# A fused two-block network on one core: the recurrence and gate columns of the second mixing stage transposed by DMA in 16-bit planes

## The chip, the cores and the metric

The program runs on one core of one Trainium2 chip. The engines in play are TensorE (matrix products and transposes), ScalarE, VectorE, GpSimd, the sync engine SP, which issues nearly all DMAs, and the 16 DMA engines of the core. The metric is the device time of one execution in microseconds (us), lower is better.

## The reference

Two transformer-like blocks run one after the other on an activation of 256 tokens by 1024 columns, all in float32. The second block is the one that matters here:

```python
h = rmsnorm_2(x, norm_mix_g)
proj = h @ w_in                                     # 1024 -> 7168 columns
q, k, v, xr, gr, g_attn, g_rnn = split(proj)        # 1024 columns each
attn_out = diff_attention(q, k, v, ...)             # 8 heads, then a norm by head
xc = conv_b + sum(xpad[:, tap:tap + S] * conv_w[tap] for tap in range(4))
r = sigmoid(blockdiag(xc, w_a) + b_a); i = sigmoid(blockdiag(xc, w_x) + b_x)
a = exp(-8 * r * softplus(-lru_lambda))
hs = scan(h_t = a_t * h_(t-1) + sqrt(1 - a_t^2) * i_t * xc_t)
rnn_out = hs * gelu(gr)
merged = sigmoid(g_attn) * (attn_out @ w_proj_attn) + sigmoid(g_rnn) * (rnn_out @ w_proj_rnn)
x = x + merged @ w_out
x = x + relu(rmsnorm_2(x) @ w_up)^2 @ w_down
```

The convolution and the scan run along the tokens. They are computed with the columns on the 128 partitions and the tokens along the free side, so `xr` and `gr`, which the projection leaves with tokens on the partitions, have to be transposed: 1024 columns each, in 128x128 blocks of 32-bit numbers.

## The kernel before

**Weights.** All weights stream through three slots, `raw[0..2]`, of 1 MB each; a slot's content is a unit, n. A float32 product is made of three reduced-precision products: ScalarE rounds `raw` to `hi`, VectorE writes `lo = raw - hi`, and TensorE adds up `xh*hi + xh*lo + xl*hi`. SP issues the load of unit n when `lo_done` shows that unit n - 3 has been split.

**The second mixing stage** is a loop over steps p = 0 to 55, written out once for each engine. Every chunk c of 512 projected columns has four steps, p = 4c to 4c + 3: two halves u of the contraction by two tiles t of 128 tokens. In each step TensorE does one `portion`, 12 matmuls of 512 columns. In the last two steps of a chunk (u = 1) ScalarE evicts the result bank `G[t]`. Chunks 0 and 3 are q, 1 and 4 are k, 2 and 5 are v, 6 and 7 the recurrence input, 8 and 9 its gate, 10 to 13 the output gates. Other work is attached to fixed steps by tables (`M2_T`, `M2_STEP`, `M2_RI`, `M2_SUB`, `M2_OUT_T`): each engine works through its own list in the order of p, and semaphores hold it where it depends on another.

**The transposes.** `M2_T` gives key (c, t) the step 4(c + 1) + 1 + t, so chunk 6 is transposed at steps 29 and 30, chunk 9 at 41 and 42. ScalarE first evicts chunk c into `hid[:, t]` (line 1105). At the step of the key, TensorE turns four 128x128 blocks of `hid` against an identity into bank `X[0]` (line 2120, a group of four), and ScalarE evicts that bank to `xrt` (lines 1066 to 1068, chunks 6 and 7) or `grt` (1070, chunks 8 and 9), counting `k_trev`.

**What hangs on them.** GpSimd computes the convolution, block b of 128 columns after block (lines 705 to 720): one scaling with bias (711), then three times a scaling into `rg` and an addition into `xc` (715, 716). It starts at `k_trev` 10, that is when both tiles of chunk 6 are in `xrt`, and needs `k_trev` 12 for blocks 4 to 7. After each block it counts `k_xc`. TensorE multiplies block b with `wax` at step 37 + b (lines 2167, 2168), so the eighth at step 44, and ScalarE makes the two sigmoids and a tanh out of it. GpSimd then computes `ig * xc` for five blocks (724), the powers that make the reciprocal roots of the attention output norm (728), and the last three products. VectorE scales `xn`, the attention output, with these (line 1679, two halves; `k_on`), TensorE transposes it from step 47 on (2177), and ScalarE and VectorE split it to `oth` and `otl`.

**Attention** runs beside this up to step 38: TensorE's scores (1930 to 1934), VectorE's bias, maximum and, two steps later, normalisation (`logits`, 1364 to 1368; 1643 to 1652), ScalarE's exponentials (1114).

**The feed-forward stages** already turn their hidden tiles by DMA: VectorE writes the high and the low 16 bits of `hid` as two planes (line 1257), SP issues a transposing DMA for each token tile (line 490), and VectorE merges the planes into 32-bit numbers (line 1265).

## Time and profile before

| | |
|---|---|
| median of 3 runs | 1007.38 us (1006.54 to 1007.86) |
| the profiled execution | 1006.67 us, span 1004.9 us |
| TensorE busy | 996.3 us (99%) |
| VectorE busy | 680.4 us (68%) |
| ScalarE busy | 545.8 us (54%) |
| GpSimd busy | 114.7 us (11%) |
| HBM read | 182.45 MB, 187 GB/s over the span with what is written |

All times in the profile count from the start of the span. In a timeline row the first number is the start, the second the duration; matmuls are pipelined, so each lasts longer than the distance to the start of the next, and distances between starts tell what a piece of TensorE's list costs. In brackets stands how long the engine had been idle and who released it. SPq rows are DMA issues. The second mixing stage lies between about 575 and 763 us, its steps 26 to 47 between 658 and 734.

### The profile page before, as it was taken

What the parts mean: (1) busy time and instruction counts of PE and PEld (TensorE: products, weight loads), DVE (VectorE), ACT (ScalarE), POOL (GpSimd) and SP (SyncE); (2) the same over time, 40 slices, a digit from 0 to 9 for tenths busy, and PEclk for the clock granted to TensorE, in tenths of its full rate; (3) what the DMA queues carried; (4) which work ended last, traced back from release to release, by engine and by line L of the source; (5) the groups of instructions that cost most, each with busy time, mean ns of one, the idle gap of its engine ahead of it and who ended that gap; (6) DMA issues with size and microseconds to landing.
All of it is one profiled execution on the core that took longest, in us unless ns stands there. A gap on an engine that the chain in (4) does not pass through costs nothing.

```text
span 1004.9 us, 12613 instructions
## 1 busy us (share of the span) xinstructions
PE 996.3 (99%) x4658; PEld 817.6 (81%) x4658; DVE 680.4 (68%) x1000; ACT 545.8 (54%) x749; POOL 114.7 (11%) x109
## 2 busy tenths in 40 slices
PE   8999999999999999999999999999999999999998
PEld 7788888888777888888888877888888888888887
DVE  6656666668977667656666668766589767656663
ACT  7444344566765546444343576766875545444441
POOL 0000000022200000000000041219923000000000
PEclk9999999999999999999999999999999999999999
DMA  8977776585434536666756376535346546787761
GB/s 266 297 241 253 238 243 213 188 302 178 129 128 138 194 127 213 225 204 207 222 187 227 123 257 210 161 133 168 126 168 209 183 156 216 231 222 228 223 196 42
DMA packets 150505, 197.77 MB, mean 197 GB/s; under 512 B 41137, under 2 KB 96570, under 8 KB 150330
## 3 DMA queue, kind: packets, MB, share of 16 engines
q1 hardware_dynamic: 150442, 197.15, 60.7%
q8 instruction: 29, 0.48, 0.2%
q14 instruction: 18, 0.15, 0.0%
q10 hardware_dynamic: 16, 0.00, 0.0%
HBM read 182.45 MB, written 5.77 MB: 187 GB/s over the span
## 4 chain that ended last, share of the span: by engine, by line
PE 93%; DVE 3%; DMA 1%; ACT 1%; POOL 1%; issue 0%; SPq 0%; ACTq 0%
PE bank L1775 22%; PE bank L1777 22%; PE bank L1776 22%; PE bank L1880 7%; PE bank L1878 7%; PE bank L1879 7%; PE bank L1788 1%; DMA raw<-in_w_in 1%; PE bank L1930 1%; PE bank L2032 1%; DVE lo L1214 1%; PE bank L2120 1%; POOL rstd_q L682 1%; PE bank L1945 0%; DMA resid<-in_x 0%; DVE ss_q L1478 0%
## 5 line engine op out<-in xcount | busy, mean ns | idle before, releaser
L1775 PE MATMUL bank<-hi,xh 128*128 128x512 f32 (+1 forms) x944 | 375.4, 398 | 1.4 <-DVE xl L1236 0.8
L1777 PE MATMUL bank<-hi,xl 128*128 128x512 f32 (+1 forms) x944 | 367.2, 389 | 0.0
L1776 PE MATMUL bank<-lo,xh 128*128 128x512 f32 (+1 forms) x944 | 366.7, 388 | 0.0
L1197 DVE TENSOR_TENSOR lo<-raw,hi 128x2048 fp32r<-128x2048 f32 x112 | 256.2, 2289 | 147.8 <-ACT hi L756 147.8
L756 ACT ACTIVATE hi<-raw 128x2048 fp32r<-128x2048 f32 (+1 forms) x116 | 220.5, 1902 | 132.9 <-PE bank L1880 96.9
L1775 PEld LDWEIGHTS bank<-hi,xh 128*128 128x128 f32 x944 | 177.5, 188 | 40.4 <-issue 2.3
L1777 PEld LDWEIGHTS bank<-hi,xl 128*128 128x128 f32 x944 | 177.3, 188 | 37.4
L1776 PEld LDWEIGHTS bank<-lo,xh 128*128 128x128 f32 x944 | 177.6, 188 | 34.4
L1214 DVE TENSOR_TENSOR lo<-raw,hi 128x1024 fp32r<-128x1024 f32 (+1 forms) x108 | 133.3, 1241 | 42.4 <-ACT hi L765 41.9
L1878 PE MATMUL bank<-hi,hh 128*128 128x512 f32 x304 | 118.9, 391 | 0.0
L1880 PE MATMUL bank<-hi,hl 128*128 128x512 f32 x304 | 118.4, 389 | 0.0
L1879 PE MATMUL bank<-lo,hh 128*128 128x512 f32 x304 | 118.3, 389 | 0.0
L765 ACT ACTIVATE hi<-raw 128x1024 fp32r<-128x1024 f32 x100 | 103.9, 1050 | 15.5 <-PE bank L1777 11.2
L830 ACT ACTIVATE hh<-hid_t 128x512 fp32r<-128x512 f32 x34 | 20.7, 629 | 92.5 <-DVE hid_t L1265 89.4
L1880 PEld LDWEIGHTS bank<-hi,hl 128*128 128x128 f32 x304 | 57.1, 188 | 11.9
L1879 PEld LDWEIGHTS bank<-lo,hh 128*128 128x128 f32 x304 | 57.1, 188 | 11.7
L1878 PEld LDWEIGHTS bank<-hi,hh 128*128 128x128 f32 x304 | 57.1, 188 | 11.5
L818 ACT ACTIVATE act_out<-bank,small 128x256 f32<-128x256 f32 x44 | 20.9, 476 | 56.4 <-PE bank L1777 53.5
L675 POOL TENSOR_TENSOR small<-small 128x1 f32<-128x1 f32 x10 | 8.5, 848 | 371.6 <-DVE small L1221 353.4
L682 POOL TENSOR_TENSOR rstd_q<-ss_q,small 128x8 f32<-128x8 f32 x16 | 37.4, 2336 | 90.7 <-DVE ss_q L1480 90.7
L1273 DVE TENSOR_TENSOR hl<-hid_t,hh 128x512 fp32r<-128x512 f32 x34 | 22.9, 691 | 20.8 <-ACT hh L830 20.8
L1248 DVE SCALAR_TENSOR_TENSOR hid<-bank,small,act_out 128x256 f32<-128x256 f32 x44 | 21.1, 481 | 15.3 <-ACT act_out L818 15.3
(257 smaller groups left out, 948.5 us busy)
## 6 DMA issues: line engine op xcount, KB each, us to landing
raw<-in_w_in SPq DMA_DIRECT2D x48, 1024.0 KB
raw<-in_ffn_w_gu SPq DMA_DIRECT2D x84, 512.0 KB
raw<-in_ffn_w_down SPq DMA_DIRECT2D x22, 1024.0 KB
raw<-in_w_up SPq DMA_DIRECT2D x16, 1024.0 KB
raw<-in_w_down SPq DMA_DIRECT2D x16, 1024.0 KB
raw<-in_w_out SPq DMA_DIRECT2D x8, 1024.0 KB
distance_table<-ftab SPq DMA_DIRECT2D x8, 576.0 KB
raw<-in_w_proj_attn SPq DMA_DIRECT2D x4, 1024.0 KB
```

The source lines that it names most:

```text
L682: nc.gpsimd.tensor_tensor(rstd_q[:, s], ss_q[:, s], minus_half[:, 0:8], ALU.pow).then_inc(rstd_sem, 1)
L756: nc.scalar.activation(hi[s][:, :, 0:width], raw[s][:, :, 0:width], ACT.Copy).then_inc(hi_done, 1)
L765: ins = nc.scalar.activation(hi[s][:, cut, :], raw[s][:, cut, :], ACT.Copy)
L1197: nc.vector.tensor_tensor(lo[s][:, :, 0:width], raw[s][:, :, 0:width], hi[s][:, :, 0:width].bitcast(F32), ALU.subtract).then_inc(lo_done, 1)
L1214: ins = nc.vector.tensor_tensor(lo[s][:, cut, 0:width], raw[s][:, cut, 0:width], hi[s][:, cut, 0:width].bitcast(F32), ALU.subtract)
L1273: nc.vector.tensor_tensor(hl[:, kt, :], hid_t[:, kt, :], hh[:, kt, :].bitcast(F32), ALU.subtract).then_inc(f.hl, 1)
L1775: nc.tensor.matmul(o, sh, wh, start=first and j == 0, stop=False)
L1776: nc.tensor.matmul(o, sh, wl, start=False, stop=False)
L1777: ins = nc.tensor.matmul(o, sl, wh, start=False, stop=last and j == 3)
L1878: nc.tensor.matmul(DB[t][h][:, :], sh, wh, start=begin, stop=False)
L1879: nc.tensor.matmul(DB[t][h][:, :], sh, wl, start=False, stop=False)
L1880: ins = nc.tensor.matmul(DB[t][h][:, :], sl, wh, start=False, stop=end)
```

## The change

For chunks 6 to 9 the transposes no longer go through TensorE. ScalarE, after evicting `hid[:, t]` and after the step's weight split, copies it once more as 16-bit elements, the low halves into one plane and the high halves into the other (`planes_of`: blocks 4 to 7 of `ig`, which are not in use yet, and `v2` for chunk 9). SP issues one transposing DMA for each tile, before the second weight load of chunk c + 3. At the step where TensorE had its group, VectorE merges the two transposed planes into `xrt` or `grt`, and counts `k_trev`. Where buffers are used again new waits order it: SP waits for the merge of the chunk before, ScalarE for it before it writes the planes of chunks 7 and 8, and before it overwrites `sq` at step 39. Three semaphores go; two were never waited for, and the wait of VectorE on itself that used the third now uses VectorE's general step counter. Left out of the diff below are their declarations.

```diff
+def by_dma(c):
+    return 6 <= c < 10
+def merged_before(c, t):
+    return 8 + 2 * (c - 7) + t + 1
+        def planes_of(c, t):
+            words = v2[:, t, 0:W] if c == 9 else ig[:, 4 + 2 * t:6 + 2 * t, :].rearrange("p b c -> p (b c)")
+            return words.bitcast(U16)
+        def turned_planes_of(c, t):
+            words = (k_2[:, 2 * t:2 * t + 2, :].rearrange("p b c -> p (b c)") if c == 9
+                     else sq if t == 0 else late_t[:, :])
+            return words.bitcast(U16).rearrange("p (k c) -> p k c", c=P)
...
 # SP
+            def flip_mixed(c):
+                for t in range(NT):
+                    sp_eng.wait_ge(k_planes, 2 * (c - 6) + t + 1)
+                    if c > 6:
+                        sp_eng.wait_ge(k_trev, merged_before(c, t))
+                    sp_eng.dma_start_transpose(turned_planes_of(c, t), planes_of(c, t)).then_inc(k_flip[t], 16)
+
             for c, (first, _) in enumerate(IN2):
                 for half in range(2):
+                    if half == 1 and by_dma(c - 3):
+                        flip_mixed(c - 3)
                     columns(a["w_in_2"], U_M2 + 2 * c + half, first, half)
...
 # ScalarE
-                if key is not None:
+                if key is not None and not by_dma(key[0]):
...
-                    elif cc < 8:
-                        nc.scalar.activation(xrt[:, 4 * (cc - 6):4 * (cc - 6) + 4,
-                                                 TAPS - 1 + tt * P:TAPS - 1 + (tt + 1) * P],
-                                             view, ACT.Copy).then_inc(k_trev, 1)
-                    else:
-                        nc.scalar.activation(grt[:, 4 * (cc - 8):4 * (cc - 8) + 4, rows], view,
-                                             ACT.Copy).then_inc(k_trev, 1)
...
                     elif kind in "xr":
-
-                        act.wait_ge(k_tr, 8 + 2 * (c - 6) + t - 1)
+                        if c == 6:
+                            act.wait_ge(k_tr, 7 + t)
                         nc.scalar.activation(hid[:, t, :], G[t][:, :], ACT.Copy, scale=rstd).then_inc(k_ev, 1)
...
                     act.wait_ge(k_oev, NH)
+                    if m == 0:
+                        act.wait_ge(k_trev, 14)
...
                 mixing_split(split_hi_part, U_M2, p)
+                if u == 1 and by_dma(c):
+                    act.wait_ge(k_ev, 2 * c + t + 1)
+                    if c in (7, 8):
+                        act.wait_ge(k_trev, merged_before(c, t))
+                    nc.scalar.activation(planes_of(c, t).rearrange("p (s c) -> p s c", s=2),
+                                         hid[:, t, :].bitcast(U16).rearrange("p (c s) -> p s c", s=2),
+                                         ACT.Copy).then_inc(k_planes, 1)
...
 # VectorE
+                key = key_at(M2_T, p)
+                if key is not None and by_dma(key[0]):
+                    cc, tt = key
+                    dve.wait_ge(k_flip[tt], 16 * (cc - 6) + 16)
+                    dst = (xrt[:, 4 * (cc - 6):4 * (cc - 6) + 4, TAPS - 1 + tt * P:TAPS - 1 + (tt + 1) * P] if cc < 8
+                           else grt[:, 4 * (cc - 8):4 * (cc - 8) + 4, tt * P:(tt + 1) * P])
+                    nc.vector.tensor_copy(dst.bitcast(U16).rearrange("p k (c s) -> p s k c", s=2),
+                                          turned_planes_of(cc, tt).rearrange("p (s k) c -> p s k c", s=2)
+                                          ).then_inc(k_trev, 1)
                 mixing_split(split_lo_half, U_M2, p)
...
 # TensorE
-                if key is not None:
+                if key is not None and not by_dma(key[0]):
...
-                    if cc < 6:
-                        pe.wait_ge(k_qn, 2 * (0, 1, 3, 4).index(cc) + tt + 1)
-                    else:
-                        pe.wait_ge(k_ev, 2 * cc + tt + 1)
+                    pe.wait_ge(k_qn, 2 * (0, 1, 3, 4).index(cc) + tt + 1)
```

VectorE's list at steps 29 and 30, in the old program. The first two rows are the end of step 29's combining; `lo<-raw,hi` are half splits of a weight unit, ISA the logits' custom operation and its read of the maximum.

```order
L1652 SCALAR_TENSOR_TENSOR l<-l,small 128x256 [waits dve_step]
L1652 SCALAR_TENSOR_TENSOR l<-l,small 128x128
L1214 TENSOR_TENSOR lo<-raw,hi 128x1024 [waits hi_half]
L1364 ISA l,small<-bank,bias 128x256 [waits k_pt,k_s]
L1364 ISA small 128x1
L1364 ISA l,small<-bank,bias 128x128
L1364 ISA small 128x1
L1368 TENSOR_SCALAR small<-small 128x2 [waits dve_step]
L1214 TENSOR_TENSOR lo<-raw,hi 128x1024 [waits hi_done]
```

The same place in the new program (its line numbers are 33 or 34 higher):

```order
L1685 SCALAR_TENSOR_TENSOR l<-l,small 128x256 [waits dve_step]
L1685 SCALAR_TENSOR_TENSOR l<-l,small 128x128
L1727 COPY xrt<-act_out 128x2x4x128 [waits k_flip0]
L1248 TENSOR_TENSOR lo<-raw,hi 128x1024 [waits hi_half]
L1398 ISA l,small<-bank,bias 128x256 [waits k_pt,k_s]
L1398 ISA small 128x1
L1398 ISA l,small<-bank,bias 128x128
L1398 ISA small 128x1
L1402 TENSOR_SCALAR small<-small 128x2 [waits dve_step]
L1727 COPY xrt<-late_t 128x2x4x128 [waits k_flip1]
L1248 TENSOR_TENSOR lo<-raw,hi 128x1024 [waits hi_done]
```

Each of the two steps has a merge into `xrt` in front of its half split. The second has the logits of step 30 in front of it.

ScalarE's list from step 26's second exponential to step 28's split, in the old program (`pt`, `xn`: evictions of attention tiles; `hid`: the eviction of chunk 6; `hi`: half splits):

```order
L1114 ACTIVATE l,small<-l,small 128x128
L765 ACTIVATE hi<-raw 128x1024
L1080 ACTIVATE xn<-bank 128x2x128 [waits k_pv]
L1105 ACTIVATE hid<-bank,small 128x512 [waits k_tr,used]
L1114 ACTIVATE l,small<-l,small 128x256 [waits k_l]
L1114 ACTIVATE l,small<-l,small 128x128
L765 ACTIVATE hi<-raw 128x1024 [waits used,raw_in1]
L1114 ACTIVATE l,small<-l,small 128x256 [waits k_l]
L1114 ACTIVATE l,small<-l,small 128x128
L765 ACTIVATE hi<-raw 128x1024
```

And in the new one:

```order
L1137 ACTIVATE l,small<-l,small 128x128
L796 ACTIVATE hi<-raw 128x1024
L1173 ACTIVATE ig<-hid 128x1024 [waits k_ev]
L1103 ACTIVATE xn<-bank 128x2x128 [waits k_pv]
L1128 ACTIVATE hid<-bank,small 128x512 [waits k_tr,used]
L1137 ACTIVATE l,small<-l,small 128x256 [waits k_l]
L1137 ACTIVATE l,small<-l,small 128x128
L796 ACTIVATE hi<-raw 128x1024 [waits used,raw_in1]
L1173 ACTIVATE ig<-hid 128x1024 [waits k_ev]
L1137 ACTIVATE l,small<-l,small 128x256 [waits k_l]
L1137 ACTIVATE l,small<-l,small 128x128
L796 ACTIVATE hi<-raw 128x1024
```

Two rows `ig<-hid` are new, each behind a half split, and all later rows move back by one and by two.

On SP four pairs of transposing DMAs now stand in the stream of loads, each pair between two loads: the first pair between those of units 18 and 19 of the stage, the next after every second load. On GpSimd nothing is moved.

## Rows read from the trace of the kernel before

**Rows 1.** The page, parts 1 and 2: engines; clock in 40 slices.

```profile
PE 996.3 (99%) x4658; PEld 817.6 (81%) x4658; DVE 680.4 (68%) x1000; ACT 545.8 (54%) x749; POOL 114.7 (11%) x109
PEclk9999999999999999999999999999999999999999
```

**Rows 2.** TensorE in order of time: start us, us, engine, line, tiles; [idle before].

```profile
580.39 0.39 PE L1775 MATMUL bank<-hi,xh 128*128 128x512 f32 x1
...
583.11 0.39 PE L1775 MATMUL bank<-hi,xh 128*128 128x512 f32 x1
...
683.76 0.60 PE L2120 MATMUL bank<-ident,hid 128*128 128x128 f32 x4
...
686.96 0.60 PE L2120 MATMUL bank<-ident,hid 128*128 128x128 f32 x4
```

**Rows 3.** GpSimd in order of time, steps 30 to 47.

```profile
673.72 0.55 POOL L711 TENSOR_SCALAR xc<-xrt,cols 128x256 f32<-128x256 f32 x1 [33.37 <-ACT xrt L1066]
...
722.26 5.53 POOL L724 TENSOR_TENSOR ig<-ig,xc 128x256 f32<-128x256 f32 x5
727.75 2.91 POOL L728 TENSOR_TENSOR rstd_q<-ss_q,small 128x16 f32<-128x16 f32 x1
```

**Rows 4.** VectorE in order of time, the scaling of `xn`.

```profile
730.69 3.44 DVE L1679 TENSOR_TENSOR xn<-xn,rstd_q 128x1024 f32<-128x1024 f32 x2 [1.26 <-POOL rstd_q L728]
```

**Rows 5.** TensorE in order of time, steps 44 and 47.

```profile
724.78 0.59 PE L2167 MATMUL bank<-xc,wax 128*128 128x256 f32 x2
...
733.85 0.60 PE L2177 MATMUL bank<-ident,xn 128*128 128x128 f32 x4
```

**Rows 6.** ScalarE in order of time, steps 27 and 28.

```profile
662.56 0.39 ACT L1080 ACTIVATE xn<-bank 128x256 f32<-128x256 f32 x1 [0.54 <-PE bank L2155]
...
666.12 1.05 ACT L765 ACTIVATE hi<-raw 128x1024 fp32r<-128x1024 f32 x1
```

**Rows 7.** VectorE in order of time, steps 28 to 30.

```profile
667.20 1.23 DVE L1214 TENSOR_TENSOR lo<-raw,hi 128x1024 fp32r<-128x1024 f32 x1 [0.31 <-ACT hi L765]
...
669.35 0.42 DVE L1364 CUSTOM_DVE_ANT_0 l<-bank,bias 128x256 f32<-128x256 f32 x1 [0.92 <-PE bank L1934]
...
672.96 0.42 DVE L1364 CUSTOM_DVE_ANT_0 l<-bank,bias 128x256 f32<-128x256 f32 x1
...
673.63 0.17 DVE L1368 TENSOR_SCALAR small<-small 128x2 f32<-128x2 f32 x1
```

**Rows 8.** Line 1265, the feed-forward stages' merge: ns min/median/max.

```profile
L1265 DVE COPY hid_t<-halves_t x27: 744/748/1345, 29.5 to 972.4; 128x1024 uint16<-128x1024 uint16 x20, 128x2048 uint16<-128x2048 uint16 x7
```

**Rows 9.** SP's queue: one load; line 490, the feed-forward transposing DMAs.

```profile
663.31 0.39 SPq L462 DMA_DIRECT2D raw<-in_w_in  x1
...
L490 SPq DMA_TRANSPOSE halves_t<-halves x54: 1188/1201/4111, 23.8 to 964.0; - x54
...
DMA to landing us min/median/max: 2.3/2.3/6.6
```

**Rows 10.** Two conv lines, then groups by line, 673 to 723 us: busy, mean.

```profile
L715 POOL TENSOR_SCALAR rg<-xrt,cols x24: 476/480/1532, 674.2 to 721.0; 128x256 f32<-128x256 f32 x24
...
L716 POOL TENSOR_TENSOR xc<-xc,rg x24: 725/739/1781, 674.8 to 721.6; 128x256 f32<-128x256 f32 x24
...
L716 POOL TENSOR_TENSOR xc<-xc,rg 128x256 f32<-128x256 f32 x24 | 21.5, 898 | 2.0
L715 POOL TENSOR_SCALAR rg<-xrt,cols 128x256 f32<-128x256 f32 x24 | 17.3, 719 | 1.6
L711 POOL TENSOR_SCALAR xc<-xrt,cols 128x256 f32<-128x256 f32 x8 | 6.5, 810 | 33.4 <-ACT xrt L1066 33.4
...
L1214 DVE TENSOR_TENSOR lo<-raw,hi 128x1024 fp32r<-128x1024 f32 x14 | 19.4, 1395 | 17.4 <-ACT hi L765 17.4
...
L1648 DVE TENSOR_SCALAR l<-l,small 128x256 f32<-128x256 f32 (+1 forms) x4 | 2.4, 646 | 0.1
L1652 DVE SCALAR_TENSOR_TENSOR l<-l,small 128x256 f32<-128x256 f32 (+1 forms) x4 | 2.1, 573 | 0.1
```

More of the change, by code:

```diff
@@ L287, in program @@
                 pt2 = sb("pt2", [P, 2, SPAN], F32, s2)
+                late_t = sb("late_t", [P, W], F32, s2)
             with scope() as s2:
@@ L366, in program @@
         m_causal = sem("m_causal")
-        m_sel = sem("m_sel")
         m_masked = sem("m_masked")
@@ L391, in program @@
         k_trev = sem("k_trev")
+        k_planes = sem("k_planes")
+        k_flip = [sem(f"k_flip{t}") for t in range(NT)]
         k_s = sem("k_s")
@@ L410, in program @@
         k_spexp = sem("k_spexp")
-        k_sp = sem("k_sp")
-        k_pad = sem("k_pad")
         k_xc = sem("k_xc")
@@ L699, in _ @@
             pool.wait_ge(n_var, 8)
-            nc.gpsimd.memset(xrt[:, :, 0:TAPS - 1], 0.0).then_inc(k_pad, 1)
+            nc.gpsimd.memset(xrt[:, :, 0:TAPS - 1], 0.0)
             norm_rstd(3)
@@ L1059, in _ @@
                     rows = slice(tt * P, (tt + 1) * P)
-                    if cc < 6:
-                        dst = q_2 if cc in (0, 3) else k_2
-                        g = C_GAIN + (4 if cc in (0, 3) else 5)
-                        nc.scalar.activation(dst[:, 4 * (cc // 3):4 * (cc // 3) + 4, rows], view, ACT.Copy,
-                                             scale=cols[:, g:g + 1]).then_inc(k_trev, 1)
-                    elif cc < 8:
-                        nc.scalar.activation(xrt[:, 4 * (cc - 6):4 * (cc - 6) + 4,
-                                                 TAPS - 1 + tt * P:TAPS - 1 + (tt + 1) * P],
-                                             view, ACT.Copy).then_inc(k_trev, 1)
-                    else:
-                        nc.scalar.activation(grt[:, 4 * (cc - 8):4 * (cc - 8) + 4, rows], view,
-                                             ACT.Copy).then_inc(k_trev, 1)
+                    dst = q_2 if cc in (0, 3) else k_2
+                    g = C_GAIN + (4 if cc in (0, 3) else 5)
+                    nc.scalar.activation(dst[:, 4 * (cc // 3):4 * (cc // 3) + 4, rows], view, ACT.Copy,
+                                         scale=cols[:, g:g + 1]).then_inc(k_trev, 1)
                 for h in range(NH):
@@ L1544, in _ @@
                 if p == M1_TOPK + TOPK // 8:
-                    nc.vector.tensor_scalar(score[:, :], score[:, :], (FILL + TAKEN) / 2, NEG,
-                                            ALU.is_gt, ALU.mult).then_inc(m_sel, 1)
+                    step(nc.vector.tensor_scalar(score[:, :], score[:, :], (FILL + TAKEN) / 2, NEG,
+                                                 ALU.is_gt, ALU.mult))
                 h = at(M1_MASK, p)
@@ L1551, in _ @@
                     if h == 0:
-                        dve.wait_ge(m_sel, 1)
                         dve.wait_ge(bias_a_in, 32)
@@ L1627, in _ @@
                     nc.vector.tensor_scalar(sp[:, 2, :], y, -LRU_C, None, ALU.mult)
-                    nc.vector.tensor_scalar(sp[:, 3, :], y, LRU_C, None, ALU.mult).then_inc(k_sp, 1)
+                    nc.vector.tensor_scalar(sp[:, 3, :], y, LRU_C, None, ALU.mult)
                 k = at(M2_STEP, p)
@@ L2114, in _ @@
                         pe.wait_ge(k_trev, order)
-                    if cc < 6:
-                        pe.wait_ge(k_qn, 2 * (0, 1, 3, 4).index(cc) + tt + 1)
-                    else:
-                        pe.wait_ge(k_ev, 2 * cc + tt + 1)
+                    pe.wait_ge(k_qn, 2 * (0, 1, 3, 4).index(cc) + tt + 1)
                     for j in range(4):
```

## The prediction, made before the result was known

> **What bounds the kernel now.** I read the page first: TensorE is busy for 99% of the span at a granted clock of 1.00 throughout [rows 1], so any instruction taken off it is worth its issue time as long as nothing else ends later. Then TensorE's own order of time, for the price of a group of four transposes: between the starts of two groups with twelve matmuls between them lie 686.96 - 683.76 = 3.20 us, and twelve matmuls without a group take 583.11 - 580.39 = 2.72 us [rows 2]. A group costs 0.48 us. Next I looked for chains that run beside TensorE and are close behind it. One stands out: GpSimd's convolution of the recurrence columns. It begins when the last `xrt` tile of column chunk 6 is there (673.72), runs eight blocks back to back until 722.26, goes on with five products, takes the powers for the output norm (727.75 to 730.66) [rows 3], and VectorE scales `xn` with them at once (730.69, two halves in 3.44 us, so the first is done at about 732.4) [rows 4]. TensorE reads the last conv block at 724.78 and the first half of `xn` at 733.85, both without a wait [rows 5]. So the chain from the eighth block to `xn` has 2.5 us of slack at step 44 and only 733.85 - 732.4 = 1.4 us at step 47. GpSimd has no free time in between: nothing of TensorE's gain can pass it unless GpSimd starts or runs earlier too.
>
> **The change part by part.**
>
> *TensorE.* Eight groups (chunks 6 to 9, two token tiles) go, at steps 29 to 42: 8 x 0.48 = 3.8 us less in its queue before step 44. This is all that the edit can give, 1006.67 - 3.8 = 1002.9 us for the profiled execution.
>
> *ScalarE.* Eight evictions of X[0] go and eight copies of 128x1024 16-bit elements come. No row shows such a copy on ScalarE; I take 1.05 us, the time of a split of 128x1024 in 32 bits [rows 6], with 0.5 us (half, were it to go by bytes) and 2.1 us (double) as ends. I let the next instruction follow 0.95 us after such a copy's start (an estimate, a little under its length). In steps 26 and 27 they come before anything is taken away: the only free time there is the 0.54 us before 662.56 [rows 6], so the first copy pushes by 0.4, the second by its 0.95, and the split of step 28 moves from 666.12 to about 667.45, ending at 668.5. VectorE's second half of that split (667.20 before, 1.23 long [rows 7]) then ends near 669.7, and the logits queued behind it start there and not at 669.35: +0.35 us. TensorE's scores for them are half a microsecond earlier and don't matter.
>
> *VectorE.* Eight merging copies come. The same copy in the feed-forward stages, 128x1024 in 16 bits, takes 0.75 us [rows 8]. The copy for (6, 0) stands before the first split of step 29, that for (6, 1) behind the logits of step 30, which began with the row at 672.96 and ended at 673.80 [rows 7]. Both lie in front of GpSimd's start, and this was the point where the old path had the TensorE group and a ScalarE eviction, started in parallel with those logits. New start: 673.80 + 0.35 + 2 x 0.75 + 0.05 for the signal = 675.7, against 673.72: **+2.0 us**. The ends are +1.2 (ScalarE's copies hidden) and +3.2 (copies of double length on ScalarE).
>
> *SP and the DMA engines.* The two transposing DMAs of a chunk stand before the second weight load of chunk c + 3. For chunk 6 the load before them is issued at 663.31 [rows 9], the first one right behind it at 663.7; the second when its planes are there, about 666.7. In the feed-forward stages an issue takes 1.2 to 4.1 us and the landing comes 2.3 to 6.6 us after it [rows 9]. With the worst of these the tiles are there at 670.3 and 673.3, before their merges at 672.3 and 674.9. The load behind them waits for the split of step 28 anyway (end 669.7) and is used five steps later. I cost the DMAs at nothing; the cover is 1.6 to 2.0 us, and each microsecond beyond it goes straight into GpSimd's start, because the split and the logits queue behind the waiting merge.
>
> *GpSimd beside VectorE.* Its 56 conv instructions would take 24 x 0.48 + 24 x 0.74 + 8 x 0.55 = 33.7 us at their undisturbed lengths; they took 17.3 + 21.5 + 6.5 = 45.3, so 11.6 us were lost. In the same stretch VectorE's splits, and its scaling and combining of `l`, all on SBUF, took 19.4 + 2.4 + 2.1 = 23.9 us [rows 10]: GpSimd lost 0.49 us for each. Six merges fall in that stretch (chunks 7 to 9), 6 x 0.75 = 4.5 us, which at 0.49 is **+2.2 us**. The ends are 0 (a one-input copy disturbs nothing) and +4.5 (each stops GpSimd for its whole length). The Trainium skill, SBUF — State Buffer, "Who interferes with whom", speaks against the change here: a VectorE copy in a two-port mode takes the port pair that GpSimd uses, for the whole instruction, and the other side stands still. The trace agrees in kind: GpSimd instructions of 0.48 us at the least last up to 1.53 [rows 10]. By the letter of that rule the term would be up to 4.5 and the time up to 1012.5 us.
>
> *The sum.* The first half of `xn` is ready at 732.4 + 2.0 + 2.2 = 736.6 and not at 732.4; TensorE wanted it at 733.85 before and would want it at 730.1 now. It starts step 47's transposes at 736.6, 2.8 us later than before, after about 6.6 us of waiting, spread over the reads of conv blocks 5, 6 and 7 (steps 42 to 44) and step 47. From there on everything keeps its distance to TensorE: VectorE's splits of steps 45 and 46 come right behind the scaling, and TensorE needs them three steps on, at least 3 x 2.72 = 8.2 us later. So 1006.67 + 2.8 = 1009.5 for an execution like the profiled one (its span of 1004.9 and 1.8 around it). The median of the three shown is 0.7 above that one, so I forecast 1007.38 + 2.8 = **1010.2 us**. The dropped semaphores and the ScalarE wait of step 39 for chunk 8's merges (queued at step 38 on VectorE, which was idle before its split) cost nothing that I can find.
>
> **Rivals.**
>
> *A. The full gain reaches the end*: 1007.4 - 3.8 = 1003.6, faster. It needs GpSimd's chain to be earlier by 3.8 - 1.4 = 2.4 us where I have it later by 4.2. For it speaks only that TensorE is the bound by every total; against it, that the chain starts behind a merge which stands behind logits, and that VectorE has no slot to make up time. It decides if the merge of (6, 1) is done before 671.3, before those logits.
>
> *B. GpSimd is late by little, and its slack covers it*: merges that cost GpSimd nothing and a start only 0 to 1.2 us later give between -1.4 and -0.2 us, or 1006.0 to 1007.2. For it: the end of 0 above; single-input copies in 16 bits were never seen beside GpSimd. Against it: the one-input scaling of `l` was stretched as well in this stretch (0.65 us mean).
>
> *C. The transposing DMAs land late*: they are issued behind a 1 MB load and beside it. If one of chunk 6 lands 11 us after its issue, VectorE holds its queue for some 2.5 us and GpSimd's start moves to +4.5: 1007.38 + 4.5 + 2.2 - 1.4 = 1012.7. For it: issues of 4.1 us when two stand together [rows 9]. Against it: DMA carries less here than in the feed-forward stages.
>
> *D. TensorE's pauses lower its granted clock.* No row of this stage shows it below 1.00 [rows 1]. Should the stretch of 10 us around steps 42 to 47 run at 1.2 GHz and not at 2.4, some 4 us would come on top: 1014.
>
> **How the numbers follow.** Forecast 0.53, A 0.07, B 0.22, C 0.13, D 0.05. The forecast's own range is 1008.5 to 1012.3 (its terms' ends, without all of them together). The range for 8 in 10 runs from 1006.0 (lower end of B; A is left out) to 1013.2 (C, with a little of the 4.5 us end of contention). What a measurement of this kernel can tell from no change is about 0.2%, 2.0 us: below 1005.4 faster, above 1009.4 slower. Faster takes A and a corner of B: 0.10. Slower takes C, D and nearly three quarters of the forecast's case: 0.57. The rest, 0.33, is within 0.2%.
>
> **What would show it.** In the new profile: TensorE without transposes of `hid` at steps 29 to 42, and with waits for `xc` (GpSimd) at the products with `wax` and for `xn` (VectorE) at step 47, together about 6.6 us; GpSimd's first conv instruction about 1.6 to 2.4 us later against the stage's start; conv instructions with a larger mean; ScalarE's copies near 1.05 us; landings of the DMAs under 6.6 us. I am wrong if TensorE shows no such waits, if GpSimd's eight blocks take no longer than 48.5 us and start no later, or if the longest new wait is one of VectorE for a DMA.

## The result, and the profile after

The changed kernel takes 1011.31 us (median of 6 runs, 1010.66 to 1012.16) against 1006.97 us of the kernel before, run beside it (6 runs, 1006.50 to 1007.86): a ratio of 1.0042 with a 95% interval of 1.0030 to 1.0055, so it is slower by some 4.3 us. The forecast was 1010.2 us, slower, with a range of 1006.0 to 1013.2.

The profiled execution took 1012.16 us, its span is 1010.4. From its page, parts 1, 2 and 4 (engines, the granted clock in 40 slices, the chain that ended last by engine), which answer to [rows 1]:

```profile
PE 997.3 (99%) x4626; PEld 816.7 (81%) x4626; DVE 685.0 (68%) x1008; ACT 549.4 (54%) x749; POOL 118.6 (12%) x109
...
PEclk9999999999999999999999999999899999999999
...
PE 86%; POOL 6%; DVE 3%; ACT 2%; DMA 1%; issue 1%; SPq 0%; ACTq 0%
```

TensorE has 32 instructions fewer and is busy for 1 us longer, and one slice of its clock is below full speed. GpSimd is busy for 3.9 us more with the same 109 instructions, and 6% of the chain that ended last runs through it. In the kernel before that share was 1%. All this points to one place, where TensorE now waits. These are the waits of TensorE (whom it waited for: us in total, times, longest), the two that concern the stage:

```profile
PE bank L2206 <- POOL xc L747: 3.4, 1, 3.4
...
PE bank L2216 <- DVE xn L1712: 0.8, 1, 0.8
```

The kernel before had neither. In order of time the first stands at step 42, the second at step 47 (start, duration, engine, line; in brackets the idle time before):

```profile
711.60 0.70 PE L2206 MATMUL bank<-xc,wax 128*128 128x256 f32 x2
...
715.11 0.39 PE L1819 MATMUL bank<-hi,xl 128*128 128x512 f32 x1
...
718.90 1.22 PE L2206 MATMUL bank<-xc,wax 128*128 128x256 f32 x2 [3.41 <-POOL xc L747]
...
725.45 0.59 PE L2206 MATMUL bank<-xc,wax 128*128 128x256 f32 x2
...
739.26 0.66 PE L2216 MATMUL bank<-ident,xn 128*128 128x128 f32 x4 [0.81 <-DVE xn L1712]
```

GpSimd, which is waited for (answers to [rows 3]):

```profile
676.55 0.55 POOL L742 TENSOR_SCALAR xc<-xrt,cols 128x256 f32<-128x256 f32 x1 [35.09 <-DVE xrt L1727]
...
688.69 2.76 POOL L742 TENSOR_SCALAR xc<-xrt,cols 128x256 f32<-128x256 f32 x1
...
734.51 2.91 POOL L759 TENSOR_TENSOR rstd_q<-ss_q,small 128x16 f32<-128x16 f32 x1
```

And the convolution's three lines with VectorE's main ones beside it, 676 to 730 us (answers to [rows 10]: busy us, mean ns):

```profile
L747 POOL TENSOR_TENSOR xc<-xc,rg 128x256 f32<-128x256 f32 x24 | 21.2, 883 | 2.0
L746 POOL TENSOR_SCALAR rg<-xrt,cols 128x256 f32<-128x256 f32 x24 | 20.3, 848 | 1.6
L742 POOL TENSOR_SCALAR xc<-xrt,cols 128x256 f32<-128x256 f32 x8 | 7.6, 956 | 35.1 <-DVE xrt L1727 35.1
...
L1248 DVE TENSOR_TENSOR lo<-raw,hi 128x1024 fp32r<-128x1024 f32 x14 | 18.1, 1295 | 16.1 <-ACT hi L796 16.0
```

The 56 instructions took 49.1 us where they took 45.3.

Two executions do not begin the stage at the same microsecond, so times are compared from its first group of transposes of `hid`, which I call the anchor. In the profile after it is

```profile
588.34 0.60 PE L2159 MATMUL bank<-ident,hid 128*128 128x128 f32 x4
```

and in the profile of before, with the `wax` products of steps 42 and 43, which will be needed too:

```profile
587.19 0.60 PE L2120 MATMUL bank<-ident,hid 128*128 128x128 f32 x4
...
717.54 0.60 PE L2167 MATMUL bank<-xc,wax 128*128 128x256 f32 x2
...
721.14 0.59 PE L2167 MATMUL bank<-xc,wax 128*128 128x256 f32 x2
```

Behind the anchor, in us (read off the timelines; "step 47" is the first group of transposes of `xn`, "convolution" runs from the start of its first instruction to the end of the 56th):

| kernel | convolution starts | its length | step 47 starts | TensorE's waits in the stage | profiled clock |
|---|---|---|---|---|---|
| before | 86.53 | 48.58 | 146.66 | none | 1.000 |
| changed | 88.21 | 52.54 | 150.92 | 3.4 + 0.8 | 0.997 |

From step 47 to the end of the span both need the same time: 1004.9 - 733.85 = 271.05 and 1010.4 - 739.26 = 271.14. The whole change is the 4.26 us by which step 47 is later: 1.7 of start, 4.0 of length, less 1.4 of slack.

### The profile page after: what moved, and what is told of

It is laid out like the page before. It is cut to its first block, busy times and chain, and to the rows that moved or that the text cites. A ratio compares the mean times of both kernels' runs of the same rounds, so it can differ in the third digit from the quotient of the medians.

```text
span 1010.4 us, 12562 instructions
## 1 busy us (share of the span) xinstructions
PE 997.3 (99%) x4626; PEld 816.7 (81%) x4626; DVE 685.0 (68%) x1008; ACT 549.4 (54%) x749; POOL 118.6 (12%) x109
## 4 chain that ended last, share of the span: by engine, by line
PE 86%; POOL 6%; DVE 3%; ACT 2%; DMA 1%; issue 1%; SPq 0%; ACTq 0%
PE bank L1817 20%; PE bank L1819 20%; PE bank L1818 20%; PE bank L1922 7%; PE bank L1920 7%; PE bank L1921 7%; POOL xc L747 2%; POOL rg L746 2%; PE bank L1830 1%; DMA raw<-in_w_in 1%; PE bank L1972 1%; POOL xc L742 1%; DVE lo L1248 1%; PE bank L2074 1%; POOL ig L755 1%
```

## The experiments

Three theories were open. **G**: GpSimd's chain sets step 47, and the convolution is longer because the merges disturb it. **D**: the transposing DMAs are to blame. **K**: TensorE's pause and its lower clock behind it are the loss. All ratios below are against the kernel before, run beside them, with 95% intervals.

### Without the transposing DMAs

```diff
-                    sp_eng.dma_start_transpose(turned_planes_of(c, t), planes_of(c, t)).then_inc(k_flip[t], 16)
-                    dve.wait_ge(k_flip[tt], 16 * (cc - 6) + 16)
+                    dve.wait_ge(k_planes, 2 * (cc - 6) + tt + 1)
```

VectorE merges the planes as they are, not turned.

> The changed kernel without the eight transposing DMAs; VectorE merges the untransposed planes at the same steps (the recurrence and gate columns hold wrong numbers). Theory (GpSimd's chain sets the end, by VectorE's merges in front of it and beside it): same as the changed kernel, +4.3 us against before, within 0.5; GpSimd's start may move by 0 to 0.3 us, the 2.1 us wait of the first gate merge goes. Rival (landing of the DMAs, their issue on SP or their traffic costs the time): +2 us or less against before.

Measured: 1011.60 us, ratio 1.0039 (1.0026 to 1.0053). The convolution starts at 88.39 and lasts 53.48, step 47 stands at 151.11. With eight DMAs fewer nothing is earlier, so D falls: neither their landing nor their writing into SBUF is in the 4.3 us. That the convolution is even 0.9 us longer is taken up under "Two dead copies".

### The powers ahead of the products

```diff
+            pool.wait_ge(k_varo, 1)
+            nc.gpsimd.tensor_tensor(rstd_q[:, 0:16], ss_q[:, 0:16], minus_half[:, 0:16],
+                                    ALU.pow).then_inc(k_rstdo, 1)
             for b in range(8):
...
-                if b == 4:
-                    pool.wait_ge(k_varo, 1)
...
```

> The changed kernel with GpSimd's powers for the output norm put directly behind the convolution, ahead of the five products. Theory: the end is set at step 47 by conv + products + powers, and behind that by the eighth conv block at step 44 alone, which was ready 3.3 us later than before against the stage: +3.3 us against before, 1.0 less than the changed kernel, and no wait for xn at step 47. Rival (what counts is the pause of 3.4 us at step 42 and the low clock after it, or anything before step 44): no change, +4.3.

Measured: 1011.15 us, ratio 1.0038 (1.0024 to 1.0052). The powers stand 5.4 us earlier (140.77 after the anchor, not 146.17), TensorE no longer waits for `xn`, and yet step 47 comes only 0.9 us earlier, at 150.03 (1.0 had been expected). The median of 1011.15 is 3.9 us above before, where 3.3 had been expected, and can hardly be told from the changed kernel's. The reason is a second path of the same length. The convolution ends at 140.81, TensorE can do the eighth `wax` product only then, and from that product to step 47 it has 733.85 - 724.78 = 9.07 us of its own work [rows 5]: 140.81 + 9.07 = 149.9. The end of the convolution holds TensorE on two ways: by the powers and `xn`, with 1.4 us of slack in the kernel before, and by the eighth product, with 724.78 - 722.30 = 2.5 us. The powers lie on only one of them.

### A late GpSimd in the kernel before

```diff
+            pool.wait_ge(k_trev, 10)
+            for _ in range(10):
+                step(nc.gpsimd.tensor_scalar(rg[:, 0, :], xrt[:, 0, 0:SEQ], 1.0, 0.0, ALU.mult, ALU.add))
             for b in range(8):
```

> The kernel before with ten dead scalings of 128x256 (0.48 us each, 0.56 from start to start, each waited for) on GpSimd in front of the convolution: nothing else is changed. Theory (GpSimd's chain has 1.4 us of slack at step 47 and nothing behind it gives time back): 5.6 us plus 0.5 to 1.5 of port time lost make +4.5 to +5.5 us, with TensorE waiting for xc and for xn. Rival (a late conv alone is absorbed, and the changed kernel's loss has another cause): under +1.5 us.

Measured: 1012.67 us, ratio 1.0052 (1.0038 to 1.0065). In GpSimd's timeline the ten take

```profile
674.81 5.75 POOL L706 TENSOR_SCALAR rg<-xrt 128x256 f32<-128x256 f32 x10 [33.33 <-ACT xrt L1069]
```

The convolution starts at 92.32 (+5.79) and lasts 49.1 (+0.5); less the slack of 1.4 that is +4.9. Step 47 is at 151.65, +5.0, and the time is 5.4 us above the 1007.30 of the kernel before beside it. Nothing was touched but GpSimd: the chain and its slack are as the prediction had them.

### TensorE kept busy through its pause

```diff
+                    if b == 5:
+                        for _ in range(8):
+                            nc.tensor.matmul(X[0][:, 0:SEQ], ident[:, :], wax[:, 0, 0:2, :]...,
+                                             start=True, stop=True)
```

in the changed kernel, ahead of the wait for block 5.

> The changed kernel with eight dead products of 128x256 in 32 bits (0.43 us each, 3.5 us) on TensorE at step 42, just where it waits 3.4 us for the sixth conv block. Theory (the low clock after the pause is hidden under GpSimd's chain): the granted clock stays at 1.00, the waits move to steps 43, 44 and 47, time as in the changed kernel within 0.4 us (+4.3 against before). Rival (the low clock is a part of the loss): 1 to 2.2 us faster than the changed kernel, +2.1 to +3.3.

Measured: 1011.30 us, ratio 1.0040 (1.0027 to 1.0054), clock 1.000. The windows of 2 us about the pause (busy us of PE, PEld, DVE, ACT, POOL; granted clock; DMA share, GB/s), first of the changed kernel:

```profile
718.00:720.00 2.00, 1.10 (x3) 0.92 (x4) 0.30 (x1) 0.00 (x0) 1.92 (x4) 0.52 0.00 1
720.00:722.00 2.00, 2.00 (x6) 1.59 (x5) 0.00 (x0) 0.95 (x3) 1.82 (x3) 0.50 0.00 0
722.00:724.00 2.00, 2.00 (x6) 1.56 (x5) 0.63 (x1) 1.34 (x2) 1.82 (x4) 0.50 0.00 0
724.00:726.00 2.00, 2.00 (x8) 1.62 (x8) 0.59 (x1) 0.35 (x1) 1.92 (x3) 0.77 0.14 14
```

and then with the filling matmuls:

```profile
718.00:720.00 2.00, 2.00 (x9) 1.43 (x8) 0.00 (x0) 0.48 (x1) 1.92 (x4) 1.00 0.00 0
720.00:722.00 2.00, 2.00 (x10) 1.50 (x8) 0.13 (x1) 1.82 (x3) 1.72 (x4) 1.00 0.00 0
```

The half clock (1.2 GHz) is gone, the time is not: K falls for the changed kernel (for the gate alone, next, it does not). The read of block 6 follows that of block 5 after 6.55 us at the low clock, and after 721.14 - 717.54 = 3.60 in the kernel before, but the 2.95 us were time in which TensorE would have waited for GpSimd anyway.

### The gate alone, the recurrence alone

```diff
-    return 6 <= c < 10
+    return 8 <= c < 10          # the other run: 6 <= c < 8
```

with the waits and evictions of the chunks that stay on TensorE restored.

> Only the gate chunks 8 and 9 turned by DMA, the recurrence chunks 6 and 7 by TensorE as before. Theory: GpSimd starts as before (86.5 us after the stage's first transpose group), its conv is longer by four merges at the 0.66 us each that the changed kernel's six cost (4.0 / 6), so +2.6; less the slack of 1.4 at step 47: +1.2 us against before, in spite of 1.9 us less on TensorE. Rival (the loss comes with the late start alone, merges in the conv are harmless): -1.0 to -1.4 us.

> Only the recurrence chunks 6 and 7 turned by DMA, the gate chunks by TensorE as before. Theory: GpSimd starts 1.7 us later, its conv meets two merges (1.3 us), less 1.4 us of slack: +1.6 us against before. Rival (merges in the conv are harmless): +0.3; rival (start harmless): 0.

Measured: gate alone 1010.30 us, ratio 1.0026 (1.0016 to 1.0035); recurrence alone 1010.73, ratio 1.0030 (1.0019 to 1.0041). The start was as I had expected: with the gate alone, which has no merge ahead of the convolution, 86.41 after the anchor, as before; with the recurrence alone 88.22, as in the changed kernel. So the +1.7 is the two merges of chunk 6 in front of GpSimd's start. The lengths were a miss: 52.58 with four merges beside the convolution and 51.54 with two, +4.0 and +3.0, where +2.6 and +1.3 had been expected. The times came out 3.2 and 3.7 us above the 1007.06 of the kernel before beside them, and +1.2 and +1.6 had been expected. Three things stand behind these misses.

The first is the path. In both runs TensorE waited for the eighth block and not for `xn`, because products and powers took 6.3 us and not 8.4: no half split of VectorE fell beside the products, where two had in the kernel before (at 721.69 and 724.57). So the slack that counts is the 2.5 us of the eighth block: 4.0 - 0.1 - 2.5 = 1.4 us of loss for the gate alone, and 1.7 + 3.0 - 2.5 = 2.2 for the recurrence alone.

The second is the clock. The executions of each kernel fall into two groups. Gate alone: three at a granted clock of 1.000 took 1007.94 to 1008.47 us, seven at 0.998 took 1010.14 to 1011.20. Recurrence alone: three at 1.000 or 0.999 took 1008.67 to 1009.50, four at 0.998 took 1010.73 to 1011.53. The trace of the gate alone is of an execution at 0.998 (1010.14), that of the recurrence alone of one at 1.000 (1009.28). From the gate alone, the eighth product, step 47, and the clock between them:

```profile
726.69 1.22 PE L2224 MATMUL bank<-xc,wax 128*128 128x256 f32 x2 [2.51 <-POOL xc L752]
...
737.32 0.60 PE L2234 MATMUL bank<-ident,xn 128*128 128x128 f32 x4
```

```profile
728.00:730.00 2.00, 2.00 (x6) 1.57 (x6) 0.00 (x0) 1.17 (x3) 2.00 (x3) 0.56 0.00 0
```

and the eighth product of the recurrence alone, whose clock stays at 1.00 and whose step 47 stands at 736.48:

```profile
727.32 0.70 PE L2224 MATMUL bank<-xc,wax 128*128 128x256 f32 x2 [2.52 <-POOL xc L752]
```

With the low clock TensorE needs 10.63 us for this piece and without it 9.16, so here, behind the last wait for GpSimd, theory K holds and the clock costs 1.5 us. The executions at full clock are near what the path alone gives, +0.9 to +1.4 and +1.6 to +2.4. No trace of the other group was kept for either kernel, so it isn't shown that the clock makes up the whole 2 us between the groups. Nor is it settled what decides: a pause of 2.51 us had the low clock behind it, and one of 2.52 us had not.

The third is the length itself, which doesn't simply add up by merges; the run with two dead copies below goes after that.

### Dead copies, and dead reductions, in the kernel before

On VectorE, at the keys of chunks 7 to 9, TensorE turning as before:

```diff
+                    nc.vector.tensor_copy(spare..., wax[:, 0, 0:4, :].bitcast(U16)...)     # one run
+                    nc.vector.tensor_reduce(spare[:, 0:6], wax[:, 0, 0:6, 0:96], AX.X, ALU.add)  # the other
```

> The kernel before with six dead 16-bit copies of 128x1024 elements, SBUF to SBUF, on VectorE at the steps of the keys of chunks 7 to 9; TensorE, ScalarE, SP and GpSimd are as before. Theory (each copy stops GpSimd, 0.66 us): conv 4.0 us longer, 52.5 instead of 48.6, +2.6 us in time. Rival (copies don't stop GpSimd; what lengthened the conv is VectorE's and ScalarE's altered timing): conv under 49.5, no change in time.

> As the run with six dead copies, but with reductions of 128x576 32-bit elements (one input, about 0.75 us) in their place, which take VectorE's time alike. Theory (GpSimd is stopped by copies in VectorE's fast mode on SBUF, not by VectorE's time): conv 48.6 within 0.7, no change in time (within 0.4). Rival (VectorE's later splits are what costs): as with the copies, +2.6 us.

Measured: copies 1010.40 us, ratio 1.0029 (1.0017 to 1.0042), 3.3 us above before (2.6 expected); reductions 1007.08, ratio 0.9999 (0.9990 to 1.0008), no difference, as expected. From the groups by line, 672 to 728 us, first with the copies:

```profile
L717 POOL TENSOR_TENSOR xc<-xc,rg 128x256 f32<-128x256 f32 x24 | 22.0, 916 | 2.0
L716 POOL TENSOR_SCALAR rg<-xrt,cols 128x256 f32<-128x256 f32 x24 | 21.0, 877 | 1.6
L712 POOL TENSOR_SCALAR xc<-xrt,cols 128x256 f32<-128x256 f32 x8 | 7.1, 888 | 33.4 <-ACT xrt L1067 33.4
...
L1696 DVE COPY spare<-wax 128x1024 uint16<-128x1024 uint16 x6 | 4.5, 749 | 0.0
```

and with the reductions:

```profile
L717 POOL TENSOR_TENSOR xc<-xc,rg 128x256 f32<-128x256 f32 x24 | 19.7, 822 | 2.0
L716 POOL TENSOR_SCALAR rg<-xrt,cols 128x256 f32<-128x256 f32 x24 | 19.1, 795 | 1.6
L712 POOL TENSOR_SCALAR xc<-xrt,cols 128x256 f32<-128x256 f32 x8 | 6.5, 809 | 33.4 <-ACT xrt L1067 33.4
...
L1696 DVE TENSOR_REDUCE spare<-wax 128x6 f32<-128x576 f32 x6 | 4.4, 739 | 0.0
```

Both keep VectorE busy for the same 4.4 to 4.5 us at the same places. The reductions leave the convolution at 48.58 us, to a hundredth what it was; the copies make it 53.44 (52.5 expected). This is the cleanest pair of the study: not VectorE's time, but the kind of its instruction is what GpSimd pays for. The Trainium skill, SBUF — State Buffer, "Who interferes with whom", says that copies can take the port pair that GpSimd needs and that a `tensor_reduce` on this chip never does. These two runs agree with both.

### Two dead copies

The same with the copies at the keys of chunk 7 alone.

> The kernel before with two dead 16-bit copies on VectorE (the two at the keys of chunk 7; the run with six had them at chunks 7, 8 and 9). Theory A (each copy costs GpSimd the same, 4.9 us over 6 = 0.8 us): convolution 48.6 + 1.6 = 50.2 us, time +0.2 us (1.6 less the slack of 1.4) over the kernel before, 1007.2. Theory B (the first copies cost most: they set in motion that VectorE and GpSimd run against each other for the rest of the convolution, and what comes later adds little): convolution 51 to 52 us, as in the run with the two merges of the recurrence's second half (51.5), time +1 to +2 us.

Measured: 1007.60 us, ratio 1.0006 (0.9997 to 1.0015); convolution 50.36 us (+1.78), step 47 at 147.04 (+0.4: the 1.4 of slack took the rest). Theory A's figure for the length fits (50.2), B's (51 to 52) doesn't; the time is 0.8 us above before, with an interval that holds no change. But A's figure fits by luck, for the 1.78 us are not all the copies'. These are GpSimd's last scaling in the kernel before, the same one with two copies, and VectorE beside the latter:

```profile
721.01 0.48 POOL L715 TENSOR_SCALAR rg<-xrt,cols 128x256 f32<-128x256 f32 x1
```

```profile
722.68 1.38 POOL L716 TENSOR_SCALAR rg<-xrt,cols 128x256 f32<-128x256 f32 x1
```

```profile
722.49 1.22 DVE L1215 TENSOR_TENSOR lo<-raw,hi 128x1024 fp32r<-128x1024 f32 x1 [1.27 <-ACT hi L766]
```

Up to there the convolution with the copies is 48.16 - 47.29 = 0.87 us behind (from its start in each): 0.44 us for a copy. The other 0.9 come with this one scaling, which a half split of VectorE stretches. In the kernel before the same split begins at 721.69, when the last addition is already running, and stretches the products behind the convolution. So what counts is how many half splits lie wholly in the convolution. Counted in each profile, those begun before its end and those over by then:

| kernel | half splits begun | over | copies or merges | length, us | over before |
|---|---|---|---|---|---|
| merges on ScalarE (below) | 11 | 11 | 0 | 47.45 | -1.1 |
| before; six reductions | 13 | 12 | 0 | 48.58 | 0 |
| late GpSimd | 13 | 12 | 0 | 49.10 | 0.5 |
| gate late (below) | 14 | 13 | 0 | 49.75 | 1.2 |
| two dead copies | 13 | 13 | 2 | 50.36 | 1.8 |
| changed | 14 | 13 | 6 | 52.54 | 4.0 |
| recurrence alone | 14 | 14 | 2 | 51.54 | 3.0 |
| gate alone | 14 | 14 | 4 | 52.58 | 4.0 |
| changed, filling matmuls | 14 | 14 | 6 | 53.20 | 4.6 |
| six dead copies | 14 | 14 | 6 | 53.44 | 4.9 |
| changed, without DMAs | 14 | 14 | 6 | 53.48 | 4.9 |

Without copies the length goes 47.45, 48.58, 49.75 with eleven, twelve and thirteen whole splits: 1.15 us for each, nearly a split's own 1.2. (The run with the late GpSimd lies 0.5 us off.) Taking 1.15 off for each split beyond twelve leaves 0.3 us for a copy or merge in the two kernels with two of them (0.44 by the rows above), 0.4 with four, and 0.4 to 0.5 with six. A longer convolution, or a TensorE that is ahead, takes a further split in, and that costs more than a copy. This is a reading of the table, one execution for each line, and not shown by a run that moves a split alone.

### The gate alone, and late

```diff
-M2_T = {(c, t): 4 * (c + 1) + 1 + t ...
+M2_T = {(c, t): 4 * (c + 1) + 1 + t if c < 8 else 46 + 2 * (c - 8) + t ...
-    return 6 <= c < 10
+    return 8 <= c < 10
```

The merges stand at steps 46 to 49, the powers ahead of the products.

> The changed kernel in which only the gate columns (chunks 8 and 9) go by DMA; their merges stand at steps 46 to 49, behind the convolution, and the powers ahead of the products. The recurrence's columns are turned on TensorE as before. Theory (the merges cost only because they fall into the convolution and ahead of its start): convolution 48.6 us, start as before (86.5 us after the anchor), TensorE 4 x 0.48 = 1.9 us less work and no wait, time 1005.1 us (1004.3 to 1006.5). Rival (the merges at the late steps stand in front of what VectorE does for step 47, or the gate's use waits for the late DMA): TensorE waits 1 to 3 us behind step 45, time 1006.5 to 1009.

Measured: 1007.61 us, ratio 1.0009 (1.0000 to 1.0018). My main expectation (48.6 us and 1005.1) was missed. Start 86.53 as expected, length 49.75 (a split more), step 47 at 145.51: 1.15 us earlier than before. It was lost again behind, as the rival said: from step 47 to the end of the span it needs 1005.6 - 732.79 = 272.8 us, 1.8 more than the kernel before. Half of that is a wait of TensorE for VectorE's `gates`. In the 5 us ahead of it VectorE is busy for 4.96, and in the kernel before for 3.64 (the wait, then the window with the gate late, then the same one before, columns as above); what the other half is isn't shown.

```profile
PE bank L1829 <- DVE gates L1709: 0.9, 1, 0.9
```

```profile
740.00:745.00 5.00, 5.00 (x26) 4.11 (x24) 4.96 (x7) 3.54 (x7) 0.00 (x0) 1.00 0.56 185
```

```profile
740.00:745.00 5.00, 5.00 (x25) 4.15 (x24) 3.64 (x5) 4.42 (x8) 0.00 (x0) 1.00 0.85 317
```

### The merges on ScalarE

```diff
-                    nc.vector.tensor_copy(dst..., turned_planes_of(cc, tt)...).then_inc(k_trev, 1)
+                    nc.scalar.activation(dst..., turned_planes_of(cc, tt)..., ACT.Copy).then_inc(k_trev, 1)
```

at the head of the key's step in ScalarE's list; and the same with the powers ahead of the products.

> The changed kernel with the eight merges on ScalarE, at the head of the step of their key, instead of on VectorE; all else (DMAs, splits of the planes, no turn on TensorE) as in the changed kernel. Theory (VectorE's 16-bit copies take GpSimd's port, and nothing else makes the convolution longer): GpSimd's convolution goes back from 52.5 to about 48.6 us, while its start, which hangs on the fourth merge, stays within 1 us of the changed kernel's 88.2 us after the anchor. Step 47 then lies 3.5 to 4 us earlier in the stage than in the changed kernel (150.9), at about 147.2, and the kernel takes about 1007.6 us (1006.5 to 1008.8). Rival (the work is anyhow longer because the DMAs write into SBUF, or because VectorE is busier): convolution 52 to 53 us as in the changed kernel, time 1011. Second rival (ScalarE was the engine that had no room: eight copies of about 1 us each delay the high halves that TensorE's blocks need): convolution short, but TensorE waits on ScalarE or VectorE in steps 30 to 45, and the time stays above 1009.

> The kernel with the merges on ScalarE, and in addition GpSimd's two power instructions put ahead of the eight products instead of between them. Theory (GpSimd's chain convolution, products, powers sets step 47, and TensorE has 8 groups of 0.48 us less to do): the scaling of xn no longer follows the powers, so step 47 is set by the convolution's end and the last blocks of TensorE's own work; TensorE waits under 1 us there, and the time is 1 to 3 us under that of the kernel with the merges on ScalarE alone: about 1005 us (1003.6 to 1007), below the kernel before. Rival (the powers only move the wait to the products, as they did in the changed kernel with the powers first, where nothing was gained): same time as with the merges on ScalarE alone, 1007 to 1008.

Measured: 1011.08 us, ratio 1.0043 (1.0029 to 1.0056); with the powers first 1011.35, ratio 1.0040 (1.0027 to 1.0054). My main expectation (1007.6, and 1005 for the second) was wrong, and the second rival held. The convolution did what it should: start at 86.83, length 47.45, end 0.8 us earlier than before. But step 47 stands at 150.39. The waits of TensorE and of ScalarE in the stage say why:

```profile
PE bank L2192 <- ACT pt L1109: 3.0, 2, 2.2
PE bank L1817 <- ACT gates L1139: 1.3, 1, 1.3
```

```profile
ACT xrt L1090 <- DMA act_out<-ig: 5.5, 2, 3.9
ACT grt L1090 <- DMA act_out<-ig: 4.0, 1, 4.0
```

Behind the wait of 2.2 us TensorE's granted clock was 0.67 at 692 to 694 us and 0.50 at 694 to 696; but the two of the five executions at 1.000 took 1011.03 and 1011.92, no less than the others. A merge at the head of its step holds ScalarE's whole list until its DMA has landed, 9.5 us in three waits, and each merge takes 1.35 to 1.40 us there, against 0.75 on VectorE. With the powers first nothing was won either: they waited 7.06 us for VectorE's `ss_q`, and step 47 stands at 152.26. So the convolution was freed of the merges as the theory had it and the kernel was no faster: another engine's list had become late. No version tried beats the kernel before.

## Why the prediction was right

**TensorE.** Eight groups were to give 3.8 us. Just before its wait TensorE was 3.4 us ahead of the kernel before: the last matmul ahead of it starts at 715.11 and the next could follow at 715.34, 127.0 after the anchor, against 717.54 - 587.19 = 130.35. That is 0.42 us for a group, not 0.48. It changed nothing, since all of it was waited away.

**ScalarE's copies.** These are the rows of the split into planes and of the merges (ns min/median/max):

```profile
L1173 ACT ACTIVATE ig<-hid x6: 1041/1048/1057, 663.0 to 693.3; 128x1024 uint16<-128x1024 uint16 x6
```

```profile
L1727 DVE COPY xrt<-act_out x2: 754/756/759, 673.2 to 688.6; 128x1024 uint16<-128x1024 uint16 x2
```

1.05 and 0.75 us, both as taken. **GpSimd's start** was to be 2.0 us later and was 1.7; VectorE's list ahead of it was pushed by 0.2 and not by 0.35, and the next instruction follows 0.64 us after the first merge's start, not 0.75.

**The DMAs** were costed at nothing, and the run without them shows that this held for the time, but the cover was thinner than "landing under 6.6 us" sounds:

```profile
L636 SPq DMA_TRANSPOSE act_out<-ig x3: 1237/1242/1379, 664.9 to 693.0; - x3
L636 SPq DMA_TRANSPOSE late_t<-ig x3: 2162/2271/4054, 667.7 to 694.4; - x3
...
DMA to landing us min/median/max: 3.8/6.1/6.6
```

VectorE did wait once for one of them, 2.06 us at step 37, outside the path. Moved to ScalarE's list, ahead of what TensorE reads, the same landings cost 9.5 us of waiting.

**The contention** is the term that was mis-sized: "6 merges at 0.49 of their length, +2.2" measured +4.0, near its upper end of 4.5. By the table of half splits it is two terms. About 1.2 of the 4.0 us are no merge's but those of a thirteenth whole half split, which the prediction did not count because it took the stretch as fixed. The six merges are the other 2.8 us, 0.47 us each where 0.37 had been put. So the prediction was right about the merges in kind and nearly in size, and what it lacked was the split; the total came near the 4.5 us of the rule of the Trainium skill that it weighed (SBUF — State Buffer, "Who interferes with whom") without each merge having cost its full length. At one place VectorE leaves GpSimd no gap:

```profile
688.64 0.76 DVE L1727 COPY xrt<-act_out 128x1024 uint16<-128x1024 uint16 x1
689.30 1.20 DVE L1248 TENSOR_TENSOR lo<-raw,hi 128x1024 fp32r<-128x1024 f32 x1
690.42 0.77 DVE L1727 COPY xrt<-late_t 128x1024 uint16<-128x1024 uint16 x1
691.08 1.44 DVE L1248 TENSOR_TENSOR lo<-raw,hi 128x1024 fp32r<-128x1024 f32 x1
```

Against these the GpSimd instruction of 688.69 above, 0.55 us undisturbed, lasts 2.76 us: it ends at 691.45, a quarter of a microsecond after the second merge.

**The sum** was +2.8 and came to +4.3: 1.7 + 4.0 - 1.4. The time is only 1.1 us above the forecast, since the kernel before came out 0.4 us lower beside it (1006.97, not 1007.38); that part is luck. The products and powers between the end of the convolution and `xn` cost 8.4 us in both. **The waits** were to be 6.6 us, spread over steps 42 to 47. They are 4.2 us, and 2.95 more are hidden in the low clock; they were not spread, since the whole 3.4 us of lead was waited off at once, at step 42.

**Rivals.** A did not happen, and its condition (the second merge of chunk 6 done before 671.3) was missed by 4 us, counted from the anchor. B needed merges that cost GpSimd nothing, and fell with the length of the convolution. C fell with the run without DMAs, though its time of 1012.7 is near the result: the time alone could not have told it from the forecast. D's mechanism was there (half clock from about 718 to 725 us) and its price was not, since TensorE had nothing to be late for. In the gate alone, where the low clock came behind the last wait for GpSimd, 1.5 us were paid.

## What to carry to other kernels

An engine that is busy 99% of the time is not a bound in the sense that work taken off it comes back: first ask which chain arrives just behind it, with how much slack, and where the replacing instructions stand relative to that chain's start. Follow each chain on every way by which it reaches the bound engine, since each has a slack of its own (1.4 and 2.5 us here). Beside GpSimd's long SBUF work a VectorE copy of 0.75 us cost 0.3 to 0.5 us here, by the table; count besides what the stretch takes in when it grows, since one more half split cost 1.15. A reduction of the same length beside it costs nothing, so the pair "dead copies, dead reductions" separates the kind of instruction from VectorE's time in two runs. And before reading one trace, look whether the executions of the kernel fall into groups, and of which one it is.

## What the runs showed that was not expected

- A 3.4 us pause of TensorE, the longest of the stage, came with some 7 us at half the granted clock (0.52 at 718 to 720, 0.50 at 720 to 724, 0.77 at 724 to 726 us). Eight matmuls in the pause kept it at 1.00, without effect on the time. In the gate alone a pause of 2.51 us was followed by half clock where TensorE was the bound, and that cost 1.5 us.
- Two dead copies at 0.75 us put GpSimd back by 0.44 us each, and then by 0.9 us more, because a half split of VectorE now met the convolution's last scaling. A GpSimd instruction of 0.55 us lasted 2.76 us across two merges of VectorE and the half split between them.
- A 16-bit merge of 128x1024 takes 0.75 us on VectorE, and on ScalarE 1.35 to 1.40 with its strided output, while ScalarE's split into planes of the same size takes 1.05.
- Each way of placing the work that was tried ran into another one: GpSimd (the changed kernel), the `wax` products behind the same convolution (powers first), VectorE (gate late), ScalarE (merges there).
